# The opening of the input projections: order of VectorE's work, quarters of the first weights, dummy transposes, and 64 bytes of padding

## The chip, the cores and the metric

One core of one Trainium2 chip runs the whole kernel in one launch. The metric is the device time in microseconds of that core, as the median of three runs. A separate profiled execution gives the trace.

## The reference

An encoder layer on two sequences (256 and 1024 tokens, together T = 1280, width D = 1024), all in float32. The part that the change touches comes first: a layer norm of the input, and one wide projection of it.

```python
x = layer_norm(x, ln_in_g, ln_in_b)          # [1280, 1024]
h = x @ w_in[l]                              # [1024, 6144]
q_na, k_na, v_na, q_hg, z_f, z_b, i_hg, g_hg, gate_na, gate_hg = jnp.split(h, splits, axis=-1)
a_out = neighbourhood_attention(heads_na(q_na), heads_na(k_na), heads_na(v_na), na_rpb[l])
...
o_hg = hgrn2_bidirectional(...)
...
mix = jax.nn.sigmoid(gate_na) * a_out + jax.nn.sigmoid(gate_hg) * r_out
x = layer_norm(ALPHA * x + mix @ w_out[l], ln1_g[l], ln1_b[l])
y = expert_choice_ffn(x, w_router[l], w_gate_e[l], w_up_e[l], w_down_e[l])
x = layer_norm(ALPHA * x + y, ln2_g[l], ln2_b[l])
```

## The kernel before

The kernel is a row of stages: projections (`stage_front`), attention, recurrence, mixing and output, the choice of experts, the experts. Each stage clears its semaphores and ends in a barrier of all engines. Tensors between stages lie in DRAM. Within a stage each engine has its own program, written out by hand, and the engines meet at semaphores.

**The projections.** The tokens are NT = 10 tiles of 128 rows. The 12 blocks of 512 columns of `w_in` are called slabs; `ORDER = (2, 6, 7, 3, 4, 0, 1, 5)` are the eight that this stage computes, and j counts them. Float32 accuracy comes from splitting: each operand is rounded to a high part and the rest is its low part, and each product is three matmuls of 512 columns, high by high, high by low, low by high (L364 to L366). A tile has KD = 8 blocks of 128 along D, so `product(i)` is 24 matmuls, and a slab 240. For slabs 3, 4, 5, 0 and 1 the result is wanted turned: the weights are then the stationary operand and the tokens the moving one (L359 to L361), in units of 512, 512 and 256 tokens.

**One tile.** SP loads `x_in` (three buffers, L230). VectorE takes its statistics, `measure` (L448, two operations of 512 columns) and `gather_stats` (L453); GpSimd makes rstd from them (L325, L327); VectorE subtracts the mean and multiplies by `g` (`centre`, L457), multiplies by rstd and adds `b` (`shift`, L466). The result `y` (two buffers) is stored by SP (L240) and transposed by TensorE in eight transposes, `turn` (L341), to the PSUM tile `tp` (two). ScalarE copies the high part out, `copy_x` (L394), VectorE the low part, `low_x` (L472). Only then can `product(t)` of slab 0 start. Slabs after the first need no more of this, as all tiles are turned by then.

**Weights.** A slab comes in two halves of 1 MB (L235) to `fr_raw`. ScalarE makes the high part of a half (`weight_hi`, L383), VectorE the low part (`weight_lo`, L436). There are two buffers: that of slabs 0, 2, 4, 6 lies in a block `carry`, which is allocated from the far end of each partition's memory, right under a pad of 8 floats, `side_pad`; that of slabs 1, 3, 5, 7 in ordinary tiles (`fr_w_hi`, `fr_w_lo`). The names `x_in`, `y`, `g_all` and `b_all` lie in a tile that the trace calls `bias_table`. Later the carry block holds the first heads of the attention, and `wroom` and the routing tables are allocated from the same end.

**The order.** SP issues x tile 0, g, x tile 1, b, both halves of the weights, x tile 2; then for each t: store y(t), load x tile t + 3, the weights of slab 1 at t = 2, and the store of product(t - 2). VectorE, for each t: gather_stats(t), centre(t), measure(t + 1), shift(t), low_x(t - 1); at t = 1 the low parts of slab 0's weights follow, at t = 7 and 8 those of slab 1. TensorE: turn(0), and for each t turn(t + 1) and then product(t). ScalarE: copy_x(t), at t = 0 the high parts of slab 0, then the eviction of product(t - 1), and the high parts of slab 1 at t = 6 and 7.

Of the kernel before, what the change touches and what calls it, by code (L numbers as in the profile page):

```python
# [31 lines left out]
P = 128  # L32
D = 1024
# [125 lines left out]
def stage_front(nc, ident, x, g, b, xln, w_in, h, hT, qk, xs, ws, xT_hi, xT_lo, room, carry,  # L159
# [22 lines left out]
    with ExitStack() as ctx:  # L182
# [32 lines left out]
        def factor(i):  # L215

            return -NA_DIM ** -0.5 if ORDER[units[i][0]] == 0 else 1.0

        def late_at(i, lag):

            n = i - NT - lag
            return n // 2 if n >= 0 and n % 2 == 0 and n // 2 < LATE else None

        with nc.Block() as block:
            @block.sync
            def _(sp):
# [4 lines left out]

                def load_w(j, v):
                    if j >= 1:
                        sp.wait_ge(w_lo_done, 2 * (j - 1) + v + 1)
                    sp.dma_start(raw[:, v], w_view[:, 4 * v:4 * v + 4, ORDER[j] * SLAB:(ORDER[j] + 1) * SLAB])\  # L235
                      .then_inc(w_ready[v], 16)

# [36 lines left out]

                load_x(0)
                sp.dma_start(g_all, rows_of(g, D)).then_inc(g_ready, 16)
                load_x(1)
                sp.dma_start(b_all, rows_of(b, D)).then_inc(b_ready, 16)
                load_w(0, 0)
                load_w(0, 1)  # L280
                load_x(2)
# [53 lines left out]
            def _(pe):  # L335
                def turn(t):
# [5 lines left out]
                                                   ident[:])  # L342
                    last.then_inc(y_turned, 1)

                def product(i):
                    n, (j, t, turned) = i % NB, units[i]
                    if i >= NB:
# [3 lines left out]
                        pe.wait_ge(x_lo, t + 1)  # L351
                    to = acc[n][:, 0:width(i)]
                    for k in range(KD):
                        if t == 0 and k % 4 == 0:
                            pe.wait_ge(w_lo_done, 2 * j + k // 4 + 1)
                        if turned:
                            c, a, count = turned
                            hi, lo = w_hi[j % 2][:, k, c * P:(c + 1) * P], w_lo[j % 2][:, k, c * P:(c + 1) * P]
                            nc.tensor.matmul(to, hi, xT_hi[:, k, a:a + count], start=(k == 0), stop=False)  # L359
                            nc.tensor.matmul(to, hi, xT_lo[:, k, a:a + count], start=False, stop=False)  # L360
                            last = nc.tensor.matmul(to, lo, xT_hi[:, k, a:a + count], start=False, stop=(k == KD - 1))  # L361
                        else:
                            hi, lo = w_hi[j % 2][:, k, :], w_lo[j % 2][:, k, :]
                            nc.tensor.matmul(to, xT_hi[:, k, rows(t)], hi, start=(k == 0), stop=False)  # L364
                            nc.tensor.matmul(to, xT_hi[:, k, rows(t)], lo, start=False, stop=False)
                            last = nc.tensor.matmul(to, xT_lo[:, k, rows(t)], hi, start=False, stop=(k == KD - 1))  # L366
                    last.then_inc(mm_done, 1)

                turn(0)
                for t in range(NT):  # L370
                    if t + 1 < NT:
                        turn(t + 1)
                    product(t)
                for i in range(NT, N):
                    product(i)

            @block.scalar
            def _(act):
                def weight_hi(j, v):
                    if j >= 2 and v == 0:  # L380
                        act.wait_ge(mm_done, first[j - 1])
                    act.wait_ge(w_ready[v], 16 * j + 16)
                    nc.scalar.activation(w_hi[j % 2][:, 4 * v:4 * v + 4, :], raw[:, v], ACT.Copy).then_inc(w_hi_done, 1)  # L383

                def late_high(n):
                    act.wait_ge(late_ready, 16 * n + 16)
# [26 lines left out]
                for t in range(NT):  # L413
                    copy_x(t)
                    if t == 0:
                        weight_hi(0, 0)
                        weight_hi(0, 1)
                    if t >= 1:
                        evict(t - 1)
                    if t >= 6 and t - 6 < 2:  # L420
# [11 lines left out]
            @block.vector  # L432
            def _(dve):
                def weight_lo(j, v):
                    dve.wait_ge(w_hi_done, 2 * j + v + 1)
                    nc.vector.tensor_tensor(w_lo[j % 2][:, 4 * v:4 * v + 4, :], raw[:, v],  # L436
                                            w_hi[j % 2][:, 4 * v:4 * v + 4, :].bitcast(F32), ALU.subtract)\
                      .then_inc(w_lo_done, 1)

                def late_low(n):  # L440
# [50 lines left out]
                    else:  # L491
                        nc.vector.tensor_copy(out[:, n, 0:width(i)], src).then_inc(copied[n], 1)  # L492

                measure(0)
                for t in range(NT):
                    gather_stats(t)
                    if t == 0:
                        dve.wait_ge(g_ready, 16)
                    centre(t)
                    if t + 1 < NT:  # L500
                        measure(t + 1)
                    if t == 0:
                        dve.wait_ge(b_ready, 16)
                    shift(t)
                    if t >= 1:
                        low_x(t - 1)
                    if t == 1:
                        weight_lo(0, 0)
                        weight_lo(0, 1)
                    if 7 <= t < 9:  # L510
                        weight_lo(1, t - 7)
                low_x(NT - 1)
                for i in range(NT, N):
                    j, t, _ = units[i]
                    if 4 <= t < 6 and j + 1 < len(ORDER):
# [2290 lines left out]
def build(nc, x, ln_in_g, ln_in_b, w_in, rpb, lb_fwd, lb_bwd, norm_g, w_na, w_hg, w_out, ln1_g, ln1_b, w_router,  # L2806
# [9 lines left out]
    with ExitStack() as ctx:  # L2816
        s = Stage(nc, ctx, "main")
        ident = s.sb("ident", [P, P])
        stage_consts(nc, ident)
        ctx.enter_context(nc.sbuf_tensor("side_pad", [P, 8], F32, side="right"))  # L2820
        routing, mix = ctx.enter_context(ExitStack()), ctx.enter_context(ExitStack())
        with ExitStack() as bias:
            b = Stage(nc, bias, "bias")
# [83 lines left out]
```

## Time and profile before

| | |
|---|---|
| median of three runs | 2809.39 us (2809.33 to 2813.06) |
| the profiled execution's own time | 2808.32 us |
| its span | 2806.5 us |
| TensorE busy | 2675.0 us, 95% |
| VectorE busy | 1828.3 us, 65% |
| ScalarE busy | 1411.5 us, 50% |
| GpSimd busy | 561.3 us, 20% |
| HBM read and written | 577.46 and 105.88 MB |

The span runs from the first to the last instruction of the profiled execution; the 1.8 us to its own time lie around it. The shares are means over all stages. "Busy" on TensorE is modelled from the starts of its matmuls. Names in the rows: PE is TensorE, PEld its weight loads, DVE VectorE, ACT ScalarE, POOL GpSimd, SPq the issues of SyncE. "out<-in" names the tiles, and a bracket gives the idle time before an instruction and what ended it.

### The profile page before, as it was taken

Reading aid. Unit: us, or ns where it says so; the run is one execution under the profiler, and the core shown is the slowest. Engines: PE = TensorE matmul, PEld = TensorE weight load, DVE = VectorE, ACT = ScalarE, POOL = GpSimd, SP = SyncE. Lnnn points to the kernel's source line nnn. Section 1 sums busy time; section 2 is a strip of 40 time slices with the busy share of each in tenths; the row PEclk is TensorE's granted clock in tenths of the full one; section 3 lists DMA queues with packets and bytes.
Section 4 is the critical chain, followed back from the end, with each engine's and each line's share of the span. In section 5 each row is a group of like instructions: output and inputs, shape, how many; then the busy total and the mean of one; then the engine's idle time right before and its main releaser. Section 6 shows DMA issues by size and latency. Waiting matters only on the chain.

```text
span 2806.5 us, 44574 instructions
## 1 busy us (share of the span) xinstructions
PE 2675.0 (95%) x18224; PEld 2143.6 (76%) x18224; DVE 1828.3 (65%) x2297; ACT 1411.5 (50%) x1781; POOL 561.3 (20%) x492
## 2 busy tenths in 40 slices
PE   7999999989999979993999999999999999999998
PEld 5788888877888858882777777777777777777776
DVE  6212231768999766656776776677677677677788
ACT  2211221866556243331565566566566566556665
POOL 2001030004454334321001010110011001111334
PEclk9999999999999989995999999999999999999999
DMA  6478875666665464326688788778788788878984
GB/s 232 159 198 236 256 261 137 166 225 217 215 238 195 167 220 132 119 103 229 241 304 294 273 296 316 270 288 305 276 303 292 291 292 305 305 276 315 371 309 153
DMA packets 237452, 686.26 MB, mean 245 GB/s; under 512 B 18729, under 2 KB 65208, under 8 KB 232128
## 3 DMA queue, kind: packets, MB, share of 16 engines
q1 hardware_dynamic: 219904, 627.96, 63.3%
q0 software_dynamic: 17344, 55.44, 7.3%
q8 instruction: 145, 2.38, 0.3%
q14 instruction: 59, 0.48, 0.1%
HBM read 577.46 MB, written 105.88 MB: 243 GB/s over the span
## 4 chain that ended last, share of the span: by engine, by line
PE 49%; DMA 1%; POOL 1%; DVE 1%; issue 1%; ACT 0%; POOLq 0%; DVEq 0%; ACTq 0%
PE moe_strip L2465 11%; PE moe_down L2480 4%; PE moe_down L2481 4%; PE moe_down L2482 4%; PE moe_up L2480 4%; PE moe_gate L2480 4%; PE moe_gate L2482 4%; PE moe_gate L2481 4%; PE moe_up L2481 4%; PE moe_up L2482 4%; PE moe_up L2406 1%; PE moe_turn L2440 0%; POOL moe_minus_mean L2292 0%; DMA out<-moe_norm_x 0%; DMA y<-moe_out_p,moe_at_out 0%
## 5 line engine op out<-in xcount | busy, mean ns | idle before, releaser
L2673 DVE TENSOR_TENSOR pieces_low<-pieces_raw,moe_high 128x1024 fp32r<-128x1024 f32 x768 | 893.5, 1219 | 354.7 <-PE moe_strip L2465 344.3
L2565 ACT ACTIVATE moe_high<-pieces_raw 128x1024 fp32r<-128x1024 f32 x768 | 769.3, 1052 | 362.0 <-PE moe_up L2482 197.2
L2465 PE MATMUL moe_strip<-pieces_raw,moe_xT_p 128*32 128x256 f32 x4096 | 230.2, 383 | 1.0 <-ACT moe_xT_p L2577 1.0
L2465 PEld LDWEIGHTS moe_strip<-pieces_raw,moe_xT_p 128*32 128x32 f32 x4096 | 130.4, 111 | 96.6 <-issue 13.7
L2480 PE MATMUL moe_gate<-moe_high,moe_xT 128*128 128x512 f32 x512 | 202.3, 395 | 1.9 <-DVE pieces_low L2673 1.9
L2480 PE MATMUL moe_up<-moe_high,moe_xT 128*128 128x512 f32 x512 | 203.0, 396 | 1.2 <-DVE pieces_low L2673 1.2
L2480 PE MATMUL moe_down<-moe_high,moe_hdn 128*128 128x512 f32 x512 | 202.5, 395 | 0.0
L1030 POOL TENSOR_TENSOR hg_W<-hg_E 128x640 f32<-128x640 f32 (+1 forms) x92 | 165.8, 1829 | 179.2 <-DVE hg_E L1304 83.7
L2482 PE MATMUL moe_gate<-pieces_low,moe_xT 128*128 128x512 f32 x512 | 199.7, 390 | 0.0
L2481 PE MATMUL moe_up<-moe_high,moe_xT 128*128 128x512 f32 x512 | 199.6, 390 | 0.0
L2481 PE MATMUL moe_down<-moe_high,moe_hdn 128*128 128x512 f32 x512 | 199.5, 390 | 0.0
L2481 PE MATMUL moe_gate<-moe_high,moe_xT 128*128 128x512 f32 x512 | 199.5, 390 | 0.0
L2482 PE MATMUL moe_down<-pieces_low,moe_hdn 128*128 128x512 f32 x512 | 199.4, 389 | 0.0
L2482 PE MATMUL moe_up<-pieces_low,moe_xT 128*128 128x512 f32 x512 | 199.2, 389 | 0.0
L2256 POOL COPY moe_at_in<-main_picks 32x1 uint32<-32x1 uint32 (+1 forms) x32 | 10.4, 353 | 784.2 <-PE moe_up L2406 775.4
L1061 PE MATMUL hg_facc<-bias_fw,bias_fx 128*128 128x512 f32 x320 | 131.7, 411 | 12.0 <-PEq L103 5.4
L492 DVE COPY fr_out<-fr_acc 128x512 f32<-128x512 f32 (+1 forms) x28 | 17.7, 634 | 191.8 <-PE fr_acc L361 107.2
L1062 PE MATMUL hg_facc<-bias_fw,bias_fx 128*128 128x512 f32 x320 | 126.7, 396 | 0.0
L1063 PE MATMUL hg_facc<-bias_fw,bias_fx 128*128 128x512 f32 x320 | 126.6, 396 | 0.0
L2480 PEld LDWEIGHTS moe_up<-moe_high,moe_xT 128*128 128x128 f32 x512 | 96.0, 188 | 33.9 <-issue 13.2
L2480 PEld LDWEIGHTS moe_down<-moe_high,moe_hdn 128*128 128x128 f32 x512 | 96.1, 188 | 25.7 <-issue 6.6
L411 ACT ACTIVATE fr_out<-fr_acc 128x512 f32<-128x512 f32 (+1 forms) x38 | 21.4, 563 | 184.4 <-PE fr_acc L366 114.2
(365 smaller groups left out, 5747.4 us busy)
## 6 DMA issues: line engine op xcount, KB each, us to landing
pieces_raw<-in_w_gate_e SPq DMA_DIRECT2D x128, 1024.0 KB, 5.3
pieces_raw<-in_w_up_e SPq DMA_DIRECT2D x128, 1024.0 KB, 7.3
pieces_raw<-in_w_down_e SPq DMA_DIRECT2D x128, 1024.0 KB, 5.0
bias_fx<-xs SPq DMA_DIRECT2D x40, 1024.0 KB, 5.3
fr_raw<-in_w_in SPq DMA_DIRECT2D x16, 1024.0 KB, 9.2
ws<-fr_late_split SPq DMA_DIRECT2D x32, 512.0 KB, 4.8
bias_fw<-ws SPq DMA_DIRECT2D x32, 512.0 KB, 8.2
mo_gates<-h SPq DMA_DIRECT2D x20, 512.0 KB, 4.5
```

The source lines that it names most:

```text
L411: nc.scalar.activation(out[:, n, 0:width(i)], src, ACT.Copy).then_inc(copied[n], 1)
L1030: last = nc.gpsimd.tensor_tensor(to, a, b, ALU.subtract)
L1061: nc.tensor.matmul(f_acc[i % 2][:], fx[:, i % 2, 0, c, :], hi, start=(c == 0), stop=False)
L1062: nc.tensor.matmul(f_acc[i % 2][:], fx[:, i % 2, 0, c, :], lo, start=False, stop=False)
L1063: last = nc.tensor.matmul(f_acc[i % 2][:], fx[:, i % 2, 1, c, :], hi, start=False, stop=(c == KD - 1))
L2406: last = nc.tensor.transpose(to[:, k * P:(k + 1) * P], rows_s[:, (4 * j + k) * P:(4 * j + k + 1) * P], ident[:])
L2465: last = nc.tensor.matmul(strip_ps[j * CP:(j + 1) * CP, kind, :], x, raw[g % RAW][:, k * D + j * STRIP:k * D + (j + 1) * STRIP], start=sta ...
L2480: nc.tensor.matmul(to[:], x_k[:, kk, 0:CS], hi, start=(kk == 0), stop=False)
L2481: nc.tensor.matmul(to[:], x_k[:, kk, CS:2 * CS], hi, start=False, stop=False)
L2482: return nc.tensor.matmul(to[:], x_k[:, kk, 0:CS], lo, start=False, stop=(kk == count - 1))
L2565: nc.scalar.activation(high[:, g % HI, cols], raw[g % RAW][:, cols], ACT.Copy).then_inc(hi_done, 1)
L2673: nc.vector.tensor_tensor(low[g % RAW][:, cols], raw[g % RAW][:, cols], high[:, g % HI, cols].bitcast(F32), ALU.subtract).then_inc(lo_done, 1)
```

## The change

- VectorE's order. A tile is measured, gathered and centred in one go (`open_tile`). Tile 0 is then shifted at once; tile 1 is opened; low_x(0), two quarters of the weights' low part, shift(1), the other two quarters. Then for each t from 1: open_tile(t + 1), low_x(t), shift(t + 1). The low parts of slab 1 come after the last low_x.
- The first slab's high and low parts are made in four quarters (two blocks of 128 along D each) instead of two halves, and product(0) waits for each quarter. The counts of later waits are renumbered (`w_count`).
- TensorE transposes the identity matrix 56 times ahead of turn(0) and 28 times behind it, to a PSUM tile that nobody reads; turn(t + 1) moves from ahead of product(t) to its middle, after the first 12 matmuls.
- SP loads `b` ahead of x tile 1 instead of behind it.
- The pad at the far end grows from 8 to 24 floats, so that the carry block, and what is allocated there later, starts 64 bytes lower: at a multiple of 128 bytes, where it started 64 bytes past one.

```diff
+        def w_count(j, v):
+            return 2 * j + v + 3 if j else 2 * v + 2
...
                     if j >= 1:
-                        sp.wait_ge(w_lo_done, 2 * (j - 1) + v + 1)
+                        sp.wait_ge(w_lo_done, w_count(j - 1, v))
...
                 sp.dma_start(g_all, rows_of(g, D)).then_inc(g_ready, 16)
+                sp.dma_start(b_all, rows_of(b, D)).then_inc(b_ready, 16)
                 load_x(1)
-                sp.dma_start(b_all, rows_of(b, D)).then_inc(b_ready, 16)
                 load_w(0, 0)
...
+                def warm(count):
+                    for _ in range(count):
+                        nc.tensor.transpose(acc[NB - 1][:, 0:P], ident[:], ident[:])
...
                     for k in range(KD):
-                        if t == 0 and k % 4 == 0:
-                            pe.wait_ge(w_lo_done, 2 * j + k // 4 + 1)
+                        if j == 0 and t == 0 and k % 2 == 0:
+                            pe.wait_ge(w_lo_done, k // 2 + 1)
+                        if j >= 1 and t == 0 and k % 4 == 0:
+                            pe.wait_ge(w_lo_done, w_count(j, k // 4))
+                        if j == 0 and k == KD // 2 and t + 1 < NT:
+                            turn(t + 1)
...
+                warm(56)
                 turn(0)
-                for t in range(NT):
-                    if t + 1 < NT:
-                        turn(t + 1)
-                    product(t)
-                for i in range(NT, N):
+                warm(28)
+                for i in range(N):
                     product(i)
...
+                def first_weight_hi(q):
+                    if q % 2 == 0:
+                        act.wait_ge(w_ready[q // 2], 16)
+                    nc.scalar.activation(w_hi[0][:, 2 * q:2 * q + 2, :], raw[:, q // 2, q % 2 * 2:q % 2 * 2 + 2], ACT.Copy)\
+                      .then_inc(w_hi_done, 1)
...
                     if t == 0:
-                        weight_hi(0, 0)
-                        weight_hi(0, 1)
+                        for q in range(4):
+                            first_weight_hi(q)
...
+                def first_weight_lo(q):
+                    dve.wait_ge(w_hi_done, q + 1)
+                    nc.vector.tensor_tensor(w_lo[0][:, 2 * q:2 * q + 2, :], raw[:, q // 2, q % 2 * 2:q % 2 * 2 + 2],
+                                            w_hi[0][:, 2 * q:2 * q + 2, :].bitcast(F32), ALU.subtract)\
+                      .then_inc(w_lo_done, 1)
...
-                measure(0)
-                for t in range(NT):
+                def open_tile(t):
+                    measure(t)
                     gather_stats(t)
                     if t == 0:
                         dve.wait_ge(g_ready, 16)
                     centre(t)
-                    if t + 1 < NT:
-                        measure(t + 1)
-                    if t == 0:
-                        dve.wait_ge(b_ready, 16)
-                    shift(t)
-                    if t >= 1:
-                        low_x(t - 1)
-                    if t == 1:
-                        weight_lo(0, 0)
-                        weight_lo(0, 1)
-                    if 7 <= t < 9:
-                        weight_lo(1, t - 7)
-                low_x(NT - 1)
+
+                open_tile(0)
+                dve.wait_ge(b_ready, 16)
+                shift(0)
+                open_tile(1)
+                low_x(0)
+                first_weight_lo(0)
+                first_weight_lo(1)
+                shift(1)
+                first_weight_lo(2)
+                first_weight_lo(3)
+                for t in range(1, NT):
+                    if t + 1 < NT:
+                        open_tile(t + 1)
+                    low_x(t)
+                    if t + 1 < NT:
+                        shift(t + 1)
+                for v in range(2):
+                    weight_lo(1, v)
...
-        ctx.enter_context(nc.sbuf_tensor("side_pad", [P, 8], F32, side="right"))
+        ctx.enter_context(nc.sbuf_tensor("side_pad", [P, 24], F32, side="right"))
```

## Rows read from the trace of the kernel before

**Rows 1.** The first line of the page: span and instructions.
```profile
span 2806.5 us, 44574 instructions
```

**Rows 2.** The waits of TensorE, 0 to 600 us.
```profile
PE fr_tp L341 <- DVE bias_table L466: 20.9, 3, 12.8
PE na_s L706 <- PEq L103: 3.8, 1, 3.8
```

**Rows 3.** The timeline, 10 to 25 us: start us, us, engine, operation [idle before].
```profile
10.15 1.29 DVE L448 BATCH_NORM_STATS2 fr_stats<-bias_table 128x6 f32<-128x512 f32 x2 [0.20 <-DMA bias_table<-in_x]
11.44 1.28 DVE L466 SCALAR_TENSOR_TENSOR bias_table<-bias_table,fr_rstd 128x1024 f32<-128x1024 f32 x1
...
15.75 3.71 ACT L383 ACTIVATE carry<-fr_raw 128x2048 fp32r<-128x2048 f32 x2
18.09 1.29 DVE L448 BATCH_NORM_STATS2 fr_stats<-bias_table 128x6 f32<-128x512 f32 x2 [3.93 <-DMA bias_table<-in_x]
19.30 1.27 DVE L466 SCALAR_TENSOR_TENSOR bias_table<-bias_table,fr_rstd 128x1024 f32<-128x1024 f32 x1
...
20.62 1.97 PE L341 MATMUL fr_tp<-main_ident,bias_table 128*128 128x128 f32 x8 [5.87 <-DVE bias_table L466]
...
21.68 4.48 DVE L436 TENSOR_TENSOR carry<-fr_raw,carry 128x2048 fp32r<-128x2048 f32 x2
...
24.11 0.77 PE L364 MATMUL fr_acc<-carry,front_xT_hi 128*128 128x512 f32 x1 [1.52 <-DVE carry L436]
```

**Rows 4.** The same timeline, the first matmul that is shorter (eleven stand before it).
```profile
28.94 0.46 PE L366 MATMUL fr_acc<-carry,front_xT_lo 128*128 128x512 f32 x1
```

**Rows 5.** Busy time of a stretch: PE, PEld, DVE, ACT, POOL, granted clock, DMA, GB/s.
```profile
70.00:80.00 10.00, 7.74 (x30) 5.81 (x30) 9.14 (x11) 3.48 (x4) 2.80 (x4) 0.83 0.20 79
```

**Rows 6.** The timeline of TensorE around tile 8 (six matmuls between the last two).
```profile
70.06 0.40 PE L366 MATMUL fr_acc<-carry,front_xT_lo 128*128 128x512 f32 x1
72.71 1.31 PE L341 MATMUL fr_tp<-main_ident,bias_table 128*128 128x128 f32 x8 [2.26 <-DVE bias_table L466]
74.00 0.76 PE L364 MATMUL fr_acc<-carry,front_xT_hi 128*128 128x512 f32 x1
...
77.01 0.40 PE L365 MATMUL fr_acc<-carry,front_xT_hi 128*128 128x512 f32 x1
```

**Rows 7.** The timeline of TensorE: the first matmul of slabs 1 to 5.
```profile
92.85 0.40 PE L364 MATMUL fr_acc<-fr_w_hi,front_xT_hi 128*128 128x512 f32 x1
...
147.30 0.40 PE L364 MATMUL fr_acc<-carry,front_xT_hi 128*128 128x512 f32 x1
...
202.25 0.40 PE L359 MATMUL fr_acc<-front_xT_hi,fr_w_hi 128*128 128x512 f32 x1
...
257.39 0.40 PE L359 MATMUL fr_acc<-front_xT_hi,carry 128*128 128x512 f32 x1
...
313.08 0.40 PE L359 MATMUL fr_acc<-front_xT_hi,fr_w_hi 128*128 128x512 f32 x1
```

**Rows 8.** Issues of g, x tile 1 and b, and times to landing.
```profile
L278 SPq DMA_DIRECT2D bias_table<-in_ln_in_b x1: 432/432/432, 3.8 to 3.8; - x1
...
DMA to landing us min/median/max: 5.8/6.8/7.7
```

**Rows 9.** The timeline of one steady tile, 38 to 41 us.
```profile
38.38 1.03 PE L341 MATMUL fr_tp<-main_ident,bias_table 128*128 128x128 f32 x8
...
39.17 0.48 PE L364 MATMUL fr_acc<-carry,front_xT_hi 128*128 128x512 f32 x1
...
39.45 1.09 ACT L394 ACTIVATE front_xT_hi<-fr_tp 128x512 fp32r<-128x512 f32 x2 [0.28 <-PE fr_tp L341]
...
40.57 1.29 DVE L472 TENSOR_TENSOR front_xT_lo<-fr_tp,front_xT_hi 128x512 fp32r<-128x512 f32 x2 [0.56 <-ACT front_xT_hi L394]
```

**Rows 10.** Issues of the two halves of the first weights, and times to landing.
```profile
L235 SPq DMA_DIRECT2D fr_raw<-in_w_in x2: 555/574/592, 4.2 to 4.9; - x2
...
DMA to landing us min/median/max: 9.9/10.9/12.0
```

More of the change, by code:

```diff
@@ L434, in weight_lo @@
                 def weight_lo(j, v):
-                    dve.wait_ge(w_hi_done, 2 * j + v + 1)
+                    dve.wait_ge(w_hi_done, w_count(j, v))
                     nc.vector.tensor_tensor(w_lo[j % 2][:, 4 * v:4 * v + 4, :], raw[:, v],
                                             w_hi[j % 2][:, 4 * v:4 * v + 4, :].bitcast(F32), ALU.subtract)\
+                      .then_inc(w_lo_done, 1)
[3 more added lines that the diff above has]
+                                            w_hi[0][:, 2 * q:2 * q + 2, :].bitcast(F32), ALU.subtract)\
                       .then_inc(w_lo_done, 1)
```

## The prediction

> **What bounds the kernel now.** I read the page first, then the opening of the trace engine by engine. The span is 2806.5 us [rows 1], and every stage ends in a barrier of all engines, so a microsecond that the projections' stage ends earlier is one that everything behind it starts earlier. In this stage TensorE is the bound from its first product at 24.11 on; between that and the stage's closing barrier it has the one wait at 72.71 [rows 2, 3]. TensorE waited 20.9 us in three places for a normalised tile `y` (L466) [rows 2]: 12.8 us until the first transposes, 5.87 us before the second ones, and 2.26 us before those of tile 8 at 72.71 [rows 2, 3, 6]. The reader is to see two things beside these waits. The first 11 matmuls take 4.83 us, 24.11 to 28.94, 0.44 us each, before the spacing falls [rows 3, 4]; and after the stop at 70.06 seven matmuls take 3.01 us, with a granted clock of 0.83 in that stretch [rows 5, 6]. 0.43 us for 512 columns is the 1.2 GHz level, 0.23 us the 2.4 GHz level (in the first stretch the spacing alone tells it). From 92.85 on, the slabs follow without a gap, 54.45 to 55.69 us each [rows 7].
>
> Why `y` comes late: VectorE runs each tile's measure(t+1) between centre(t) and shift(t). shift(1) therefore waits for measure(2), that is for the landing of x tile 2 behind 2 MB of weights: measure(2) starts at 18.09, shift(1) at 19.30, turn(1) at 20.62. Then low_x(0) and both halves of the weights' low part follow, to 26.1 [rows 3]. At 70 the same engine does weight_lo(1, 0) between two tiles, and turn(8) is late by that.
>
> **The opening, step by step.** All times are worked out for the changed kernel.
> 1. `b` takes the place of x tile 1 in the queue. x tile 1 landed at 10.1 (measure(1) ended its wait for it at 10.15), `b`, issued at 3.8, 7.7 us later at 11.5 [rows 3, 8]. Both have 512 KB, so now b is there at 10.1 and x tile 1 at 11.5. centre(0) is done before that: `g`, the one that took 5.8 us, keeps its place [rows 8]. shift(0) runs 10.15 to 11.4; before it ran 11.44 to 12.7 [rows 3].
> 2. 56 dummy turns begin when the block does, about 2.4 us. In turn(1) eight took 1.97 us with the last one's end, 0.22 from start to start (1.2 GHz); in a warm stretch the product follows eight of them after 0.79 us, 0.10 each [rows 3, 9]. If the clock rises 5 us after the first one, as it did after 24.11 [rows 4], 23 go at 0.22 and 33 at 0.10: done at 10.7, before y(0). They cost nothing. turn(0) then runs 11.45 to 12.5.
> 3. copy_x(0) 12.5 to 13.6 (1.09 us, [rows 9]). The first half of the weights was issued at 4.2 and landed 9.9 us later, at 14.1, the second at 4.9 + 12.0 = 16.9 [rows 10]. Its place in the queue is the same, as the same bytes stand before it. Two halves took 3.71 us on ScalarE [rows 3]; a quarter is a quarter of that and a little fixed cost, about 1.0: high quarters done at 15.1, 16.1, 17.9, 18.9.
> 4. VectorE: measure(1) 11.5 to 12.8, aggregate and centre(1) to 14.25, low_x(0) to 15.5 (1.2 us from start to start in each case), low quarter 0 to 16.65 (a quarter of 4.48 us, [rows 3], and a little), quarter 1 to 17.8, shift(1) to 19.0, quarters 2 and 3 to 20.15 and 21.3. So the first product starts at 16.7 instead of 24.11: **7.4 us gained**. The 28 dummy turns behind turn(0) end at 15.3, before it.
> 5. Inside product(0), at 0.229 a matmul, 12 of them end at 19.45; quarter 2 is ready at 20.2: a wait of **0.75**. turn(1) stood ahead of 24.11 before and is now inside: **0.9** more (38.38 to 39.17, and 0.08 us for the change back, [rows 9]). The other 12 matmuls end at 23.85 (0.229 is the spacing of slab 2, 54.95 us for 240, [rows 7]). Tile 2, landed at 18.1, is measured 21.3 to 22.6, centred to 24.1, low_x(1) to 25.3: TensorE waits **1.5** for it.
> 6. product(0) at the full rate: 4.83 - 11 x 0.229 = **2.3 us gained**.
>
> **The stall at 70.** With weight_lo(1, v) behind the last low_x, turn(8) is on time. From 70.29 (next matmul due) to 77.01 are 6.7 us, in which a turn and 7 matmuls were done [rows 6], 0.88 + 1.6 = 2.5 us at full rate: **4.2 us gained**. Where the low parts go now they are covered: low_x(9) ends with the start of product(9), the two take 2.24 us each, and slab 1 begins 5.5 us after that start; its second half is wanted later still.
>
> **The steady tiles.** The turn of tile t+1 now stands in the middle of product(t), so turn, copy and low part must be done in the second half. From turn start to the end of low_x were 38.38 to 41.86, 3.48 us; the cover is 0.88 + 12 x 0.229 = 3.63 [rows 9]. That fits by 0.15 us, and I cost it at nothing. If ScalarE or VectorE is 0.5 us late on each of eight tiles the price is 8 x 0.35 = 2.8 us. Queued work: SP's stores of `h` stand between the loads of x, but a tile's load is issued some 12 us before it is measured, against 5.8 to 12.0 us that any of the first loads took [rows 8, 10], so SP and the two waits that the diff renumbers cost nothing. GpSimd's two operations per tile keep their order; between the aggregate and the shift there are still two operations of VectorE, as before, so their cover is the same.
>
> **The 64 bytes.** The carry block holds the weights of slabs 0, 2, 4, 6; those of 1, 3, 5, 7 lie in ordinary tiles. Like against like: slab 1 takes 54.45 us and slab 2 54.95; slab 3 55.14 and slab 4 55.69 [rows 7]. If that is the start address, four slabs gain 0.5, 0.5, 0.55, 0.55: **2.1 us**. Bounds: 0, if it is something else in these tiles; as much again, 4.2, if later stages, whose tiles on that side move too, gain like these (no row of theirs has a pair to compare). I take 2.1, as the two kinds differ in nothing else that the rows show. The Trainium skill (SBUF — State Buffer, Specifications) gives lines of 16 bytes, so that both addresses start a line and by this rule the edit brings 0; the sum would then be 10.8 instead of 12.9. The trace has a difference of 0.5 us a slab where the rule has none, so the measured one stands in the sum.
>
> **Sum.** 7.4 + 2.3 + 4.2 - 0.75 - 0.9 - 1.5 + 2.1 = 12.9 us. The profiled execution took 2808.32 us, 1.8 outside its span; less 12.9 it is 2795.4. The median of the runs is 1.1 above it (2809.39): 2796.5.
>
> **Rivals.**
> A, the sum, 0.64. Own range: 2793.5 (the 64 bytes worth 4.2, and 0.9 less waiting) to 2800 (they are worth 0, and the steady tiles lose 1.4).
> B, the clock, 0.22. Of dummy turns no row tells whether they raise it: the two turns at 12.78 and 20.62 did not. If they don't, the 56 last till 14.8, turn(0) till 16.6, the 28 till 22.8, and product(0) starts there at 0.43; its first 12 matmuls end at 27.9, turn(1) and the rest at 31.5, and product(1) starts at 31.5 instead of 25.35: 6.1 us less, 2802.6. A milder form: the waits of 0.75 and 1.5 us bring the clock down once. At 70 a stop of 2.26 us was followed by seven matmuls at 0.43, 1.4 us more, plus 0.5 on the turn: 2798.4. For it: that row. Against it: both waits are shorter than 2.26 us. The Trainium skill (TensorE: Matmul & The Clock Gate, HAM oscillation) says that a wait for data between groups of matmuls sends the clock down and lets each group begin slow; the trace agrees at 70.
> C, slower, 0.04: low_x(t+1) misses its slot because tile t+2's open_tile stands before it on VectorE and its x is not there, on every tile. It outweighs the gain when low_x starts 0.15 + 12.9/9 = 1.6 us late on each. With 2.5 us on each of nine the loss is 21 us, 8 beyond the gain: 2817.7. Against: a tile's load has 12 us for what took at most 12.0 behind two blocks of weights, and 5.8 in front of them [rows 8, 10].
> D, the gain is lost, 0.10: something else ends the stage, or half of the steps in step 4 wait for a landing. Against: TensorE has no wait from slab 1 to the closing barrier, 3.8 us [rows 2]. Time: 2806 to 2811.
>
> **How the numbers follow.** Time 2796.5. Range 2793.5 to 2804.5: A and most of B. 0.2% is 5.6 us, about what a measurement here can tell: faster is A, B and a little of D, 0.87; same 0.09; slower 0.04.
>
> **What would show it.** shift(0) at 10.15 and turn(0) at 11.5; the first product's matmul near 16.7, spaced 0.23 from the start; waits of 0.75 and 1.5 us and none after 26; no stop at 70; slab 1 starting near 81.5, slabs 2 and 4 at 54.45 and 55.14 us. Wrong it would be with a product's matmul spacing of 0.43 anywhere after 16.7, dummy turns still running at y(0)'s arrival, a wait for `front_xT_lo` on every tile, or slabs of unchanged length.

## The result and the profile after

The changed kernel took 2793.26 us (median of four runs, 2791.28 to 2795.86), the kernel before 2809.36 us: a ratio of 0.9939, 95% interval 0.9928 to 0.9951, or 16.1 us. The forecast was 2796.5 us with a range from 2793.5 to 2804.5. The time is 0.24 us below the range and the gain is 3.2 us larger than the sum. Faster was right; the size was not.

The profiled execution has a span of 2789.5 us, 17.0 less than [rows 1]. First TensorE's waits in the first 600 us (total, times, longest), which answer to [rows 2]:

```profile
PE fr_acc L351 <- PEq L103: 2.4, 1, 2.4
...
PE fr_acc L376 <- DVE front_xT_lo L494: 1.3, 1, 1.3
PE fr_acc L376 <- DVE carry L458: 1.0, 1, 1.0
PE fr_tp L345 <- DVE bias_table L488: 1.0, 1, 1.0
PE fr_tp L345 <- DVE carry L458: 0.4, 1, 0.4
```

The three waits for `y` of 20.9 us have become one of 1.0 us before turn(0); one of 1.0 us before the first product, of 0.4 us inside it and of 1.3 us before product(1) are left. The 2.4 us are the program's start, before the dummy turns. The timeline of the opening, which answers to [rows 3, 4] (start, duration, engine, operation, and the idle time before it; some rows stand for several instructions):

```profile
2.42 7.90 PE L351 MATMUL fr_acc<-main_ident 128*128 128x128 f32 x56 [2.42 <-PEq L103]
...
9.99 1.28 DVE L488 SCALAR_TENSOR_TENSOR bias_table<-bias_table,fr_rstd 128x1024 f32<-128x1024 f32 x1
...
11.34 1.09 PE L345 MATMUL fr_tp<-main_ident,bias_table 128*128 128x128 f32 x8 [1.02 <-DVE bias_table L488]
...
12.26 3.22 PE L351 MATMUL fr_acc<-main_ident 128*128 128x128 f32 x28
...
15.16 2.35 DVE L458 TENSOR_TENSOR carry<-fr_raw,carry 128x1024 fp32r<-128x1024 f32 x2
...
16.52 0.47 PE L376 MATMUL fr_acc<-carry,front_xT_hi 128*128 128x512 f32 x1 [1.04 <-DVE carry L458]
...
16.83 0.40 PE L377 MATMUL fr_acc<-carry,front_xT_hi 128*128 128x512 f32 x1
...
19.90 1.09 PE L345 MATMUL fr_tp<-main_ident,bias_table 128*128 128x128 f32 x8 [0.41 <-DVE carry L458]
...
25.00 0.50 PE L376 MATMUL fr_acc<-carry,front_xT_hi 128*128 128x512 f32 x1 [1.25 <-DVE front_xT_lo L494]
...
27.85 1.03 PE L345 MATMUL fr_tp<-main_ident,bias_table 128*128 128x128 f32 x8
```

The reader is to compare it with the forecast's steps: shift(0) at 9.99 (forecast 10.15), turn(0) at 11.34 (11.45), the first product at 16.52 (16.7), turn(1) in the middle of it at 19.90 (20.2), product(1) at 25.00 (25.35). The matmuls are 0.23 us apart from the second one on. At 70 us there is no stop, and the granted clock is 1.00 where [rows 5] has 0.83:

```profile
70.00:80.00 10.00, 10.00 (x49) 8.05 (x48) 6.01 (x6) 2.29 (x4) 1.05 (x3) 1.00 0.29 106
```

The steady tiles show a small difference. These are the turns of tiles 7 and 8:

```profile
60.08 1.04 PE L345 MATMUL fr_tp<-main_ident,bias_table 128*128 128x128 f32 x8
...
66.53 1.03 PE L345 MATMUL fr_tp<-main_ident,bias_table 128*128 128x128 f32 x8
```

From turn to turn are 6.45 us; over six tiles from 27.85 to 66.53 it is the same. With the shorter matmul that the slabs below show (54.40/240 = 0.2267 us) a tile of TensorE's own work would take 24 x 0.2267 + 0.88 = 6.32. So something else, by the order of the work the chain of turn, copy and low part, sets the pace by some 0.1 us a tile; turn_ahead below bears this out. The first matmuls of slabs 1 to 4, which answer to [rows 7]:

```profile
82.21 0.39 PE L376 MATMUL fr_acc<-fr_w_hi,front_xT_hi 128*128 128x512 f32 x1
...
136.61 0.39 PE L376 MATMUL fr_acc<-carry,front_xT_hi 128*128 128x512 f32 x1
...
191.01 0.39 PE L371 MATMUL fr_acc<-front_xT_hi,fr_w_hi 128*128 128x512 f32 x1
...
246.10 0.40 PE L371 MATMUL fr_acc<-front_xT_hi,carry 128*128 128x512 f32 x1
```

Slab 1 starts at 82.21 instead of 92.85. Slabs 1 and 2 take 54.40 us each and slab 3 55.09; slab 4 takes 55.12, as slab 5 starts at 301.22. The two kinds of buffer are alike now. The stage ends at 466.74 us, before at 479.16: 12.4 us earlier.

So 4.6 of the 17.0 us come after the stage that was changed. Half of that is in the recurrence, whose code has no edit. Its first and its last matmul before, and then after:

```profile
614.82 0.76 PE L1061 MATMUL hg_facc<-bias_fw,bias_fx 128*128 128x512 f32 x1 [5.38 <-PEq L103]
...
986.95 0.39 PE L1133 MATMUL hg_ring<-hg_S,bias_table 128*128 128x128 f32 x2
```

```profile
602.14 0.77 PE L1089 MATMUL hg_facc<-bias_fw,bias_fx 128*128 128x512 f32 x1 [5.40 <-PEq L103]
...
971.98 0.39 PE L1161 MATMUL hg_ring<-hg_S,bias_table 128*128 128x128 f32 x2
```

From the first start to the last end are 372.5 us before and 370.2 after. The experiments had to tell where that comes from.

### The profile page after: what moved, and what is told of

Its sections match the earlier page's. It is cut to its first block, busy times and chain, and to the rows that moved or that the text cites. A ratio compares the mean times of both kernels' runs of the same rounds, so it can differ in the third digit from the quotient of the medians.

```text
span 2789.5 us, 44747 instructions
## 1 busy us (share of the span) xinstructions
PE 2676.5 (96%) x18308; PEld 2148.0 (77%) x18308; DVE 1825.3 (65%) x2299; ACT 1412.2 (51%) x1783; POOL 566.6 (20%) x492
## 3 DMA queue, kind: packets, MB, share of 16 engines
q8 instruction: 145, 2.38, 0.3%
## 4 chain that ended last, share of the span: by engine, by line
PE 51%; DVE 1%; DMA 0%; POOL 0%; issue 0%; ACT 0%; DVEq 0%; ACTq 0%; POOLq 0%
PE moe_strip L2493 12%; PE moe_up L2508 4%; PE moe_down L2508 4%; PE moe_up L2509 4%; PE moe_up L2510 4%; PE moe_gate L2508 4%; PE moe_gate L2510 4%; PE moe_gate L2509 4%; PE moe_down L2509 4%; PE moe_down L2510 4%; PE moe_up L2434 1%; PE moe_turn L2468 0%; DVE pieces_low L2701 0%; PE moe_gate L2443 0%; PE moe_up L2468 0%
## 5 line engine op out<-in xcount | busy, mean ns | idle before, releaser
L2284 POOL COPY moe_at_in<-main_picks 32x1 uint32<-32x1 uint32 (+1 forms) x32 | 21.8, 707 | 783.9 <-PE moe_up L2434 774.9
L2493 PE MATMUL moe_strip<-pieces_raw,moe_hdn_p 128*32 128x256 f32 x2048 | 113.8, 380 | 0.0
```

The lines of the kernel that those rows point to most:

```text
L2284: nc.gpsimd.tensor_copy(to[n][:], picks[n][:, e:e + 1]).then_inc(at_ready, 1)
L2493: last = nc.tensor.matmul(strip_ps[j * CP:(j + 1) * CP, kind, :], x, raw[g % RAW][:, k * D + j * STRIP:k * D + (j + 1) * STRIP], start=sta ...
```

## The experiments

Two theories were written down for the rest of the gain: that the start address of the tiles at the far end pays in the later stages too (theory 1), or that the waits of the later stages fall another way (theory 2). All kernels but before_again (timed once, 2805.52 us) were timed in several rounds beside the kernel before; its median in the three sets was 2809.14, 2808.93 and 2809.61 us.

**pad_only**: the kernel before with the wider pad.

```diff
-        ctx.enter_context(nc.sbuf_tensor("side_pad", [P, 8], F32, side="right"))
+        ctx.enter_context(nc.sbuf_tensor("side_pad", [P, 24], F32, side="right"))
```

> The kernel before with the pad of 24 floats and nothing else. Theory 1, the start address of the tiles at the far end (carry, and later wroom) pays for what is not the opening: slabs 0, 2, 4, 6 each some 0.5 us shorter, so that slabs 2 and 4 take 54.4 and 55.1 us, and the recurrence (372.5 us from its first to its last matmul before) and the mixing stage (285.1 us) are shorter by about 2.3 and 0.8 us too: 5 us in all, about 2804.3. Theory 2, the later stages' shares are a matter of how their waits happen to fall: only the slabs gain, 2.1 us, 2807.3, and the recurrence and the mixing stage keep their lengths within 0.3 us. Theory 3, the page's lines of 16 bytes: nothing, 2809.4.

2806.39 us, ratio 0.999 (0.9981 to 0.9999). The first matmuls of slabs 1 to 4:

```profile
92.19 0.39 PE L364 MATMUL fr_acc<-fr_w_hi,front_xT_hi 128*128 128x512 f32 x1
...
146.59 0.39 PE L364 MATMUL fr_acc<-carry,front_xT_hi 128*128 128x512 f32 x1
...
200.99 0.39 PE L359 MATMUL fr_acc<-front_xT_hi,fr_w_hi 128*128 128x512 f32 x1
```

Slabs 1 and 2 take 54.40 us each, slab 3 55.09 and slab 4 55.12. From the start of slab 1 to that of slab 7 are 329.25 us, in the kernel before 331.04; slab 0 takes 68.24, before 68.74 (some 0.2 of the 0.5 is one slow matmul fewer). The last slab starts at 421.44, 2.45 us earlier than before and 2.1 earlier than in before_again (423.53). The recurrence took 374.3 us, 1.8 longer than before, which no theory had. The address pays in the slabs, and no gain shows in the later stages: theory 1 falls, and so does theory 3. The run compares two addresses 64 bytes apart. That the multiple of 128 bytes is what counts, and not the place relative to the other operand, it doesn't show.

**opening_only**: the changed kernel with the pad of 8 floats.

> The changed kernel with the old pad of 8 floats. Theory 1: the opening alone, slab 1 starting 10.2 us before 92.85 (at 82.7), the recurrence and the mixing stage as long as before (372.5 and 285.1 us): 2798 to 2799. Theory 2: the recurrence is shorter all the same, 2795.5. The slabs whose weights lie in the carry block take 54.95 and 55.69 us under both.

2793.93 us, ratio 0.9946 (0.9933 to 0.996). Slab 1 starts at 82.10, no later than with the new address (82.21, and 82.01 in after_again), so the address gives nothing in slab 0 here; slabs 2 and 4 take 54.95 and 55.69 us again. The recurrence took 369.1 us: short without the address. Theory 2 is left.

**before_again** and **after_again**: both kernels once more, as controls of how far a stage's length moves from one execution to another.

> The kernel before, once more, as a control of how far the lengths of the later stages differ between two executions of one program. Theory 1: recurrence 372.5, mixing 285.1 us within 0.3 us. Theory 2: either may be 1 us or more off.

> The changed kernel once more on this chip, timed beside the two halves of the change. Both theories: 2793 within 2 us, slab 1 at 82.2 us. Theory 1: recurrence 370.2 and mixing 284.4 us within 0.3; theory 2: 1 us or more off.

The recurrence: 372.6 and 369.5 us (372.5 and 370.2 in the first executions). The mixing stage: 282.8 and 284.2 us (285.1 and 284.4). after_again had a median of 2792.58 us, ratio 0.9942 (0.9928 to 0.9955). So the recurrence's difference is there again, while the mixing stage differs by 2.3 us between two executions of one program, and what it seemed to gain is nothing to explain.

**before_84_turns, before_128_turns, no_dummies**. What both short recurrences have is a TensorE program with 168 instructions more. In the profile page's list of queues, instructions arrive by two queues of their own, in 145 packets of 2.38 MB together and 59 of 0.48 MB. For the 44574 instructions of [rows 1] that is 64 bytes each. The page has 18224 matmuls and as many weight loads, 2.33 MB at this size, so the larger queue is TensorE's; a packet of it has 16 KB, a block of 256 instructions. A new theory, F: it matters where in the work the fetches of these blocks fall.

```diff
+                warm(56)
                 turn(0)
+                warm(28)
                 for t in range(NT):
```

> The kernel before with the 84 dummy transposes alone (56 ahead of turn(0), 28 behind it; 168 instructions more on TensorE). In the opening: the first 11 matmuls of product(0) at 0.23 instead of 0.43 us if the clock outlasts the 5 us without work before turn(1), 2.3 us gained, and nothing if it doesn't. In the recurrence two theories part. Theory F, fetch: each block of TensorE's instructions is fetched at another point of the work, as the stream is longer by 168, so the recurrence takes 369 to 370.5 us, as in the changed kernel: 2803 to 2806. Theory O, order: what shortens it comes from the other edits, so that it stays at 372.5.

2805.68 us, ratio 0.9991 (0.9982 to 1.0). The recurrence took 369.9 us, as theory F has it. In the opening the dummies gave nothing. A stretch of TensorE (busy times of PE, PEld, DVE, ACT, POOL, granted clock, DMA) and its timeline:

```profile
20.00:30.00 10.00, 7.04 (x22) 5.58 (x23) 9.96 (x11) 1.08 (x2) 1.88 (x2) 0.66 0.31 107
```

```profile
20.56 1.09 PE L341 MATMUL fr_tp<-main_ident,bias_table 128*128 128x128 f32 x8 [2.02 <-DVE bias_table L472]
24.05 0.77 PE L368 MATMUL fr_acc<-carry,front_xT_hi 128*128 128x512 f32 x1 [2.40 <-DVE carry L442]
```

The clock had been up (0.10 us a turn at 20.56), fell in the waits around turn(1) (a granted 0.66 in this stretch), and the first product ran at 0.43 us a matmul as before. Slab 1 began at 93.37.

```diff
+                warm(60)
                 turn(0)
+                warm(60)
                 for t in range(NT):
                     if t + 1 < NT:
                         turn(t + 1)
+                    if t == 0:
+                        warm(8)
                     product(t)
```

> The kernel before with 128 dummy transposes (60 ahead of turn(0), 60 behind it, 8 behind turn(1)): 256 instructions more on TensorE, which is one fetched block of 16 KB if an instruction has 64 bytes. Theory F: the fetches fall where they fell before, the recurrence takes 372.5 us. If the number of dummies or the warmer engine mattered and not where the blocks begin, it takes 369 to 370.5 as with 84. Theory O: 372.5.

2808.54 us, ratio 0.9998 (0.9989 to 1.0007): no gain, though its first product ran at the full rate and slab 1 began at 91.51. The recurrence took 376.1 us. That it isn't short is as theory F has it, as are the places of the fetches (below); that it is 3.5 us longer than 372.5 theory F doesn't say.

```diff
-                warm(56)
                 turn(0)
-                warm(28)
```

> The changed kernel without its 84 dummy transposes. Price of the clock: turn(0) takes 2 us instead of 1.1 and product(0) runs at 0.43 until some 5 us after its first matmul near 17.6; product(1) then starts about 3 us later, near 28 instead of 25, so slab 1 starts near 85 instead of 82. Theory F: the recurrence goes back to 372.5 us, and the median is 2793 + 3 + 3 = 2799. Theory O: the recurrence stays at 369 to 370.5 and the median is 2796.

2796.08 us, ratio 0.9958 (0.9945 to 0.9972): without the dummies the time lies inside the forecast range. The recurrence is back at 374.6 us. The surprise is the opening: slab 1 starts at 82.40, 0.2 us behind the changed kernel, not 3. Its timeline and TensorE's waits up to 470 us:

```profile
11.00 1.97 PE L345 MATMUL fr_tp<-main_ident,bias_table 128*128 128x128 f32 x8 [11.00 <-DVE bias_table L486]
16.69 0.77 PE L376 MATMUL fr_acc<-carry,front_xT_hi 128*128 128x512 f32 x1 [3.72 <-DVE carry L456]
...
19.39 0.54 PE L376 MATMUL fr_acc<-carry,front_xT_hi 128*128 128x512 f32 x1
19.77 0.40 PE L377 MATMUL fr_acc<-carry,front_xT_hi 128*128 128x512 f32 x1
...
25.16 0.50 PE L376 MATMUL fr_acc<-carry,front_xT_hi 128*128 128x512 f32 x1 [0.41 <-DVE front_xT_lo L492]
```

```profile
PE fr_acc L376 <- DVE carry L456: 3.7, 1, 3.7
PE fr_acc L376 <- DVE front_xT_lo L492: 0.4, 1, 0.4
```

Six matmuls run slowly and a seventh in part (16.69 to 19.77), 1.4 us more than at the full rate, yet product(1) starts at 25.16 instead of 25.00. The 1.4 us are taken out of the waits: 0.4 is left of the 1.3 before product(1), and none inside product(0). VectorE's low_x(1) sets that start in both.

**late_low_only**: of the whole change only the low parts of slab 1 moved.

```diff
-                    if 7 <= t < 9:
-                        weight_lo(1, t - 7)
                 low_x(NT - 1)
+                for v in range(2):
+                    weight_lo(1, v)
```

> The kernel before with the low parts of slab 1's weights moved behind the last low_x and nothing else. By the prediction's step: no wait ahead of turn(8), no matmul at 0.43 there, slab 1 starts 4.2 us earlier, at 88.6; the recurrence at 372.5 under both theories. A rival: the next late instruction on VectorE takes half of it back (86 to 87 would be more than forecast, 90.5 or later this rival).

2803.66 us, ratio 0.9984 (0.9975 to 0.9993), and slab 1 starts here:

```profile
87.67 0.40 PE L364 MATMUL fr_acc<-fr_w_hi,front_xT_hi 128*128 128x512 f32 x1
```

5.2 us before [rows 7]. In this execution six matmuls of product(0) were slow and a seventh in part, instead of eleven, which is 1.0 us of it. The stall at 70 was worth 4.2. The recurrence took 373.0 us.

**count_42, count_106**: the changed kernel with other numbers of dummies, 42 + 0 and 62 + 44.

```diff
-                warm(56)
+                warm(62)
                 turn(0)
-                warm(28)
+                warm(44)
```

> The changed kernel with 42 dummy transposes, all ahead of turn(0): 84 instructions more on TensorE than without dummies, 84 fewer than with 84 dummies. In the opening nothing lost: slab 1 at 82.0 to 82.6, as without any. Theory F (the fetches of TensorE's instruction blocks decide in the recurrence): the fetch that falls 127.5 us behind the recurrence's first matmul without dummies and 134.5 us with 84 lies between them, and the recurrence has a length of its own between 369 and 376 us. If it is the dummies as such, and not where the blocks begin, it is halfway at most: 371 to 373.

> The changed kernel with 106 dummy transposes (62 ahead of turn(0), 44 behind it): 212 instructions more than without dummies. Slab 1 at 82.0 to 82.8. Theory F: the fetches lie another 44 instructions later than with 84 dummies, so the recurrence may differ from 369.5 as well, by steps of 0.5 to 2 us; that it stays within 0.5 us of it would say that only the fetch at 127.5 matters, which stays away from it.

2795.44 us (ratio 0.9948, 0.9934 to 0.9961) with a recurrence of 374.5, and 2793.91 us (0.9944, 0.9931 to 0.9958) with 370.7. Slab 1 at 81.97 and 81.87. 42 dummies are not halfway: the recurrence is as long as without any. With 106 it is 0.7 us longer than the mean of the six executions with 84 (below).

**b_behind**: x tile 1 ahead of `b`, as before.

```diff
-                sp.dma_start(b_all, rows_of(b, D)).then_inc(b_ready, 16)
                 load_x(1)
+                sp.dma_start(b_all, rows_of(b, D)).then_inc(b_ready, 16)
```

> The changed kernel with b behind x tile 1 in SP's queue, as before. Step 1 of the prediction: shift(0) starts at 11.4 instead of 10.0, and as all of VectorE's opening stands behind it, the first product's matmul moves from 16.5 to 17.8 and slab 1 from 82.2 to 83.5: 1.3 us slower, 2794 to 2794.5. A rival, that the second half of the weights' landing (16.6) sets the end of the opening in both: under 0.4 us.

2794.74 us, ratio 0.9946 (0.9933 to 0.996). shift(0), the first product and slab 1:

```profile
11.24 1.28 DVE L488 SCALAR_TENSOR_TENSOR bias_table<-bias_table,fr_rstd 128x1024 f32<-128x1024 f32 x1 [1.55 <-DMA bias_table<-in_ln_in_b]
...
17.77 0.47 PE L376 MATMUL fr_acc<-carry,front_xT_hi 128*128 128x512 f32 x1 [1.03 <-DVE carry L458]
...
83.48 0.39 PE L376 MATMUL fr_acc<-fr_w_hi,front_xT_hi 128*128 128x512 f32 x1
```

Each 1.25 us later: step 1, as it was worked out.

**turn_ahead**: turn(t + 1) ahead of product(t), as before.

```diff
-                        if j == 0 and k == KD // 2 and t + 1 < NT:
-                            turn(t + 1)
...
                 for i in range(N):
+                    if i + 1 < NT:
+                        turn(i + 1)
                     product(i)
```

> The changed kernel with turn(t+1) ahead of product(t), as before. turn(1) waits for shift(1) (18.7), so product(0) starts near 19.7 and has no waits inside: it ends at 25.2. Then turn(2) waits for shift(2), 26.1, and product(1) starts at 27.1 instead of 25.0, without a turn inside: slab 1 1.2 us later, 83.4. Rival: the steady tiles win it back, as with the turn in the middle each runs by the chain of turn, copy and low part and not by TensorE (6.45 us a tile in the changed kernel against 6.39 before); then slab 1 is at 82.9 or earlier.

2794.39 us, ratio 0.9948 (0.9934 to 0.9961). The first product and slab 1:

```profile
19.95 0.78 PE L374 MATMUL fr_acc<-carry,front_xT_hi 128*128 128x512 f32 x1
...
82.61 0.39 PE L374 MATMUL fr_acc<-fr_w_hi,front_xT_hi 128*128 128x512 f32 x1
```

The start loses 3.4 us, slab 1 only 0.4 (82.61 against 82.21). Of the 3.0 us between, 0.9 are turn(1), which no longer stands inside product(0), and 1.7 the two waits of 0.4 and 1.3 us that are gone. Against them stand 0.8 us: TensorE waited 2.9 us before turn(1), the clock was down behind it (a granted 0.80 from 16 to 20 us), and the first four matmuls took 0.43 us each. The steady tiles give back some 0.8, as from turn to turn they take 6.35 us here (26.37 to 70.83, seven tiles) and not 6.45; about 0.4 is not accounted for. The rival was right.

**What the fetches do.** The same two places were read in all fourteen traces, the stores of `o` some 126 and some 210 us into the recurrence. VectorE waits for their landing, to write the buffer again. The kernel before at the first place, the queues in the 5 us from that store on, the store's landing time, VectorE, and the subtraction that GpSimd runs meanwhile:

```profile
q1 hardware_dynamic: 1392, 1.15, 78.5%
q8 instruction: 1, 0.02, 1.2%
```

```profile
L986 SPq DMA_DIRECT2D o<-bias_table x1: 371/371/371, 740.0 to 740.0; - x1
...
DMA to landing us min/median/max: 5.1/5.1/5.1
```

```profile
745.14 1.62 DVE L1338 TENSOR_TENSOR bias_table<-hg_l,main_ident 128x512 f32<-128x512 f32 x3 [1.25 <-PE hg_l L1094]
746.68 1.50 DVE L1313 TENSOR_TENSOR hg_W<-hg_E 128x640 f32<-128x640 f32 x1
...
746.22 1.29 POOL L1030 TENSOR_TENSOR hg_W<-hg_E 128x640 f32<-128x640 f32 x1
```

And before_84_turns, the same:

```profile
q1 hardware_dynamic: 1395, 1.16, 79.7%
```

```profile
L992 SPq DMA_DIRECT2D o<-bias_table x1: 371/371/371, 740.8 to 740.8; - x1
...
DMA to landing us min/median/max: 4.3/4.3/4.3
```

```profile
745.18 1.62 DVE L1344 TENSOR_TENSOR bias_table<-hg_l,main_ident 128x512 f32<-128x512 f32 x3 [0.54 <-DMA o<-bias_table]
746.72 0.97 DVE L1319 TENSOR_TENSOR hg_W<-hg_E 128x640 f32<-128x640 f32 x1
...
745.74 1.26 POOL L1036 TENSOR_TENSOR hg_W<-hg_E 128x640 f32<-128x640 f32 x1
```

In the first there is one packet in the queue of instructions: a block is fetched among these transfers and the store lands 5.1 us after its issue; in the second there is none and it lands after 4.3. How the one delays the other can be read from the store's sixteen parts, which report their landing one by one: in the kernel before fifteen are there 3.9 to 4.4 us after the issue, the sixteenth after 5.05, and the fetched packet took 0.96 us. It is so in all twelve cases with a fetch: fifteen parts on time, the last one 0.5 to 1.2 us behind them.

VectorE starts 0.7 us later (an idle 1.25 instead of 0.54; 740.0 and 5.1 give 745.1, so the landing ends the wait in the first too, though the bracket names TensorE). Its next subtraction (L1313, L1319) then takes 1.50 instead of 0.97 us, as it runs against GpSimd's. That is the port that both share: the Trainium skill (SBUF — State Buffer, Terms) says that of the two one blocks the other for a whole instruction. The trace agrees: alone this subtraction takes 0.82 us, and here it ends 0.68 us after the end of the subtraction that GpSimd was in, in both kernels (748.18 after 747.50, 747.69 after 747.01). In the kernel before it came late and fell behind GpSimd's next one. Together the fetch costs 1.3 us here, one subtraction of GpSimd.

At the second place it is the same. The wait for the store in the kernel before, and in before_84_turns:

```profile
831.01 1.62 DVE L1338 TENSOR_TENSOR bias_table<-hg_l,main_ident 128x512 f32<-128x512 f32 x3 [1.53 <-DMA o<-bias_table]
```

```profile
829.37 1.62 DVE L1344 TENSOR_TENSOR bias_table<-hg_l,main_ident 128x512 f32<-128x512 f32 x3 [0.42 <-DMA o<-bias_table]
```

Set beside before_84_turns, VectorE falls back by 1.26 to 1.30 us at the first place and by 1.26 to 1.28 at the second (1.9 in before_128_turns) in each of the six kernels with 0 or 128 dummies, and by nothing in the others with 84 or with 106. (count_42 falls back by 1.5 us at the second place without a fetch.) All executions (a fetch: within 5 us of the store's issue, the same answer at both places in every row):

| kernel | dummies | recurrence, us | a fetch in the 5 us | first store landed after, us | second store, us | median, us |
|---|---|---|---|---|---|---|
| before | 0 | 372.5 | yes | 5.1 | 5.4 | 2809.36 |
| before_again | 0 | 372.6 | yes | 5.0 | 5.1 | |
| late_low_only | 0 | 373.0 | yes | 5.0 | 5.1 | 2803.66 |
| pad_only | 0 | 374.3 | yes | 5.1 | 5.1 | 2806.39 |
| no_dummies | 0 | 374.6 | yes | 4.9 | 5.1 | 2796.08 |
| before_128_turns | 128 | 376.1 | yes | 5.0 | 5.4 | 2808.54 |
| count_42 | 42 | 374.5 | no | 4.4 | 4.2 | 2795.44 |
| before_84_turns | 84 | 369.9 | no | 4.3 | 4.2 | 2805.68 |
| opening_only | 84 | 369.1 | no | 4.4 | 4.2 | 2793.93 |
| after | 84 | 370.2 | no | 4.3 | 4.2 | 2793.26 |
| after_again | 84 | 369.5 | no | 4.4 | 4.3 | 2792.58 |
| b_behind | 84 | 369.9 | no | 4.4 | 4.2 | 2794.74 |
| turn_ahead | 84 | 371.6 | no | 4.3 | 4.2 | 2794.39 |
| count_106 | 106 | 370.7 | no | 4.3 | 4.2 | 2793.91 |

Fourteen of fourteen agree: where a fetch falls there the store lands late, and nowhere else. The six with 84 dummies average 370.0 us, the six with 0 or 128 373.8: 3.8 us, of which 2.5 are followed to two fetches. 128 dummies are 256 instructions, one whole block, and the fetches lie where they lay without any. count_42 has the short waits and is long nevertheless, so other places count as well.

## Why the prediction was off

1. **Steps 1 to 5 of the opening were right.** Every start came within 0.35 us, and the edit that was undone moved the start of slab 1 as step 1 says: `b` ahead of x tile 1 is 1.25 us, and the waits inside product(0) and before product(1) (0.4 and 1.3, forecast 0.75 and 1.5) are there.
2. **Step 6, the 2.3 us for product(0) at the full rate, was the right number for the wrong cause.** The sum to the start of slab 1 without it would be short, but the dummy turns don't earn it: without them slab 1 starts 0.2 us later. What earns it is that product(1) starts when low_x(1) is done, and a slow product(0) fits into the waits ahead of that: the sum took the 2.3 us and the waits of 0.75 and 1.5 as independent, and they are not. 84 dummies are worth 0.2 to 0.4 us in the stage that they stand in. That the number came out was luck. Rival B's 6.1 us had the dummies themselves run at the slow rate, to 22.8 us; they did not (7.90 and 3.22 us, done at 15.5), so its condition never arose and its price is not tested. Where 84 or 106 dummies stood in the changed kernel, product(0) ran at 0.23 us a matmul, but for turn_ahead. Where 42 or none did, its first six matmuls were slow and slab 1 started at 81.97 and 82.40, against 82.21 and 82.01 with 84. In turn_ahead no wait follows product(0), and four slow matmuls cost their full 0.8 us.
3. **The stall at 70**: forecast 4.2, measured 4.2 (late_low_only).
4. **The steady tiles, costed at nothing, cost 0.1 us each**, some 0.8 us in all: 6.45 us from turn to turn, 6.35 in turn_ahead. With the forecast's other terms slab 1 was due at 81.6 (92.85 less 10.75 and 0.5); it started at 82.2 and 82.0.
5. **The 64 bytes**: forecast 2.1 us, measured 1.7 to 1.8 in the changed kernel: 0.55, 0.57 and 0.57 in slabs 2, 4 and 6, and from the start of slab 1 to the stage's end 384.5 us against 386.3 in opening_only. In slab 0 the forecast 0.5 did not come, as there a tile takes 6.45 us with either address; in pad_only, where TensorE sets the pace, some 0.3 of it was there. The upper bound of 4.2 had later stages gain as well; they do not. By the lines of 16 bytes that the Trainium skill has (SBUF — State Buffer, Specifications) it would be 0. The measured 0.55 us a slab decides.
6. **The step that failed is the first paragraph's**: "a microsecond that the projections' stage ends earlier is one that everything behind it starts earlier", taken to mean that the later stages keep their length. The stage gave 12.4 us of the forecast 12.9. The recurrence gave 2.3 more in the profiled execution, and 3.8 on average over twelve, because 168 instructions more on TensorE moved every later fetch of its instructions; 2.5 of the 3.8 are two fetches that no longer fall on a store that VectorE waits for. With the 12.4 us that makes 16.2, and the median gained 16.1: this is the 3.2 us by which it was missed. No term of the sum and no bound held it, and the range ended at 2793.5.

What stays open: what the other 1.3 us are. VectorE falls back by another 1.3 near 300 us in the six kernels with 0 or 128 dummies, but in count_42 and count_106 too, and the store there does not land late. Open is also why three kernels with a fetch at both places have a recurrence 1.3 to 3.6 us longer (374.3, 374.6, 376.1) than the other three (372.5, 372.6, 373.0). In those, and in count_42 and turn_ahead, a jump of about 1.6 us falls between 175 and 190 us into the recurrence, where a subtraction of VectorE meets GpSimd's in another order; that the meeting makes the jump was read and not tried. The rest of the difference between the profiled executions, 2.3 us in attention, mixing and experts, is within what two executions of one program differ by.

## What to carry to other kernels

A slow clock costs only where TensorE sets the pace: look at what the next wait is for before you buy dummy work. An edit that adds instructions to an engine's program moves all its later fetches, and in a stage full of transfers and of meetings between VectorE and GpSimd that is worth some microseconds of either sign; a control with the same number of instructions tells it from the edit's own effect. The start address of a large matmul operand that is read hundreds of times is worth a trial: here 64 bytes made 1% of a slab. And a gain on an engine that does not set the pace, like the address in slab 0, is not collected.

## What the hardware showed that was not expected

- 240 matmuls took 54.40 us with their weights at one start address as moving operand, and 54.95 us with them 64 bytes off it: 2.3 ns each. As stationary operand 55.12 against 55.69 us for 288 matmuls. By the kernel's layout the better one is a multiple of 128 bytes; that this is the condition was not tried.
- A fetch of one 16 KB block of instructions in a burst of loads delayed one of a store's sixteen parts, and with it the landing from 4.3-4.4 to 4.9-5.1 us at one place and from 4.2 to 5.1-5.4 at another. The engine that waited lost 1.3 us each time, as it fell behind one more subtraction of GpSimd (1.26 to 1.30 us).
- In before_84_turns the clock was up for turn(1) at 20.56 (eight turns in 1.09 us) and down again for product(0) at 24.05, after idle times of 2.0 and 2.4 us on TensorE with those eight turns between them; the 28 dummies behind turn(0) took 4.14 us where the changed kernel's took 3.22; after idle times of 1.0 and 1.3 us in the changed kernel it was not down, and after one of 2.9 us in turn_ahead it was.
